# Chunk inverse of an RWKV-7 mixer: levels on diagonal 32x32 blocks, the last level as corner products

## The reference

```
sa = einsum('bhij,bhj->bhi', S, -kk_t)
S  = S * w_t + sa[..., None] * (kk_t * a_t) + v_t[..., None] * k_t
y  = einsum('bhij,bhj->bhi', S, r_t)
```

## Time and profile before

| | |
|---|---|
| median of the runs | 1234.13 us |
| profiled execution | 1235.34 us, of which the span 1233.5 us |
| PE busy, weight loads busy | 1101.8 us (89%), 803.3 us (65%) |
| DVE, ACT, POOL busy | 520.1, 301.7, 132.5 us |
| mean granted TensorE clock | 0.952 of full speed |
| instructions | 25771 |

### The profile page before, as it was taken

The page is one execution under the profiler, slowest core; times in us unless marked ns, Lnnn a source line. Parts: engine busy times, 40 slices in busy tenths (PEclk is TensorE's granted clock), DMA queues, the critical chain, the costliest instruction groups (busy, mean ns, idle before and its releaser), DMA issues.

```text
span 1233.5 us, 25771 instructions
## 1 busy us (share of the span) xinstructions
PE 1101.8 (89%) x11555; PEld 803.3 (65%) x11555; DVE 520.1 (42%) x906; ACT 301.7 (24%) x565; POOL 132.5 (11%) x154
## 2 busy tenths in 40 slices
PE   3469999999999999999787796999999999999994
PEld 1247777868686877778563283888585666665563
DVE  0693346454545445454646906120211254543104
ACT  1103131232322222312202113122211344443011
POOL 0261010010100000100102411000000000100010
PEclk9779999999999999999998898899999899999897
DMA  9400103030302121120506138022211122423001
GB/s 353 180 1 1 70 11 133 2 141 2 141 3 91 53 72 71 33 111 2 206 19 247 54 137 339 32 79 80 90 69 52 69 76 97 172 87 137 1 1 69
DMA packets 18014, 110.46 MB, mean 90 GB/s; under 512 B 6888, under 2 KB 9712, under 8 KB 11760
## 3 DMA queue, kind: packets, MB, share of 16 engines
q1 hardware_dynamic: 10640, 84.57, 18.2%
q0 software_dynamic: 2304, 20.97, 4.5%
q10 hardware_dynamic: 4960, 3.27, 0.9%
HBM read 103.35 MB, written 5.19 MB: 88 GB/s over the span
## 4 chain that ended last, share of the span: by engine, by line
PE 76%; DVE 14%; issue 5%; ACT 3%; DMA 2%; SPq 0%; ACTq 0%; DVEq 0%
PE pj L949 19%; PE bk L1053 9%; PE pj L1370 7%; PE pj L1301 5%; PE pj L1427 3%; DVE XM L1728 3%; PE pj L1297 2%; PE bk L1399 2%; PE bk L1480 2%; PE bk L879 2%; DMA ring<-in_ada 2%; PE bk L1464 1%; PE bk L1465 1%; PE bk L1014 1%; PE bk L1309 1%
## 5 line engine op out<-in xcount | busy, mean ns | idle before, releaser
L949 PE MATMUL pj<-XM,ring 128*128 128x260 f32 x1024 | 256.0, 396 | 7.8 <-DVE XM L1728 7.8
L949 PEld LDWEIGHTS pj<-XM,ring 128*128 128x128 f32 x1024 | 187.2, 191 | 47.5 <-issue 18.6
L1053 PE MATMUL bk<-arena,ring 64*64 64x64 f32 x2560 | 92.7, 222 | 6.3 <-DVE arena L1807 5.5
L1053 PEld LDWEIGHTS bk<-arena,ring 64*64 64x64 f32 x2560 | 81.8, 136 | 24.8 <-issue 15.8
L1370 PE MATMUL pj<-XM,ring 128*128 128x260 f32 x352 | 80.6, 393 | 0.0
L1370 PEld LDWEIGHTS pj<-XM,ring 128*128 128x128 f32 x352 | 68.8, 196 | 11.0
L1813 DVE TENSOR_TENSOR arena<-arena,bk 128x512 f32<-128x512 f32 x40 | 27.5, 688 | 107.6 <-PE bk L1053 107.6
L879 PE MATMUL bk<-ring,cT 128*9 128x512 f32 x240 | 35.1, 685 | 19.6 <-DMA ring<-in_ada 19.6
L1945 DVE TENSOR_SCALAR arena<-bk 128x512 f32<-128x512 f32 x4 | 2.8, 691 | 105.5 <-PE bk L1323 73.7
L2025 DVE TENSOR_TENSOR bk<-bk,arena 128x128 f32<-128x128 f32 x32 | 9.6, 299 | 72.5 <-PE bk L1465 37.3
L1728 DVE SCALAR_TENSOR_TENSOR XM<-R,vecs 128x520 f32<-128x520 f32 x40 | 38.8, 1040 | 0.2
(11 more groups left out here) (343 smaller groups left out, 1854.6 us busy)
## 6 DMA issues: line engine op xcount, KB each, us to landing
ring<-in_ada SPq DMA_DIRECT2D x16, 2048.0 KB, 8.4
ring<-in_w_in SPq DMA_DIRECT2D x8, 2048.0 KB, 7.3
ring<-in_b_w_in SPq DMA_DIRECT2D x3, 2048.0 KB, 16.1
R<-in_xT SPq DMA_DIRECT2D x2, 2080.0 KB, 13.4
ring<-in_w_out SPq DMA_DIRECT2D x2, 2048.0 KB, 8.3
ring<-in_w_q SPq DMA_DIRECT2D x2, 1536.0 KB, 6.4
out_y<-R SPq DMA_DIRECT2D x4, 520.0 KB, 2.7
XM<-in_Sd SPq DMA_DIRECT2D x1, 2048.0 KB, 17.4
```

Of the source, the lines that this page charges most:

```text
L949: last = mm(pj[:, s, a, 0:HALF], w[:, e, k, :], XM[:, e, k, a * HALF:(a + 1) * HALF], start=(k == 0), stop=(k == KT - 1))
L1053: last = mm(bk[r, out, b * C:(b + 1) * C], lhsT[r, b, :], rhs_[r, b, :], start=True, stop=True)
```

## The change

The levels run to a block size of 32 only, and on the diagonal 32x32 blocks alone. The 16 matrices of 64x64 have 32 such blocks; they lie as 128 partitions by 8 blocks of 32 columns, four in the partitions. T and Tm of the levels are `Tq` and `Tm` (256 columns in place of 512), Z is `Zq`. `blocks` now makes 32 matmuls of 32x32 by 32 columns, on the four array tiles of the diagonal. There are four levels (2, 4, 8, 16), each with both products.

The last level is made from corners: `corner_z` multiplies the off-diagonal corner of M with the lower inverted block, DVE negates it, `corner_t` multiplies the upper inverted block with it and, with an identity, also moves the lower block to its place; DVE copies both into the right half of `Tt`, and ACT copies the upper blocks into its left half (`corner`, semaphore `s_Tc`). The other corner of `Tt` is zeroed once at the start. The half projection that stood in level 4 stands between `corner_z` and `corner_t`, and the "cum" part of DVE's preparation of the next pair between DVE's two corner steps.

`chunk_products` and `plain_products` are written in parts, so that the 32x32 blocks come out at the partitions and columns where the levels read them; the masks follow, and one constant, `idq`, is loaded more.

Core of the diff:

```diff
-LEVELS = (2, 4, 8, 16, 32)
+LEVELS = (2, 4, 8, 16)
+QC = 32
...
+            def corner(m):
+                act.wait_ge(s_Te, (NLEV + 2) * m + NLEV + 1)
+                for cp in range(2):
+                    lo = slice(cp * C, cp * C + QC)
+                    last = A(Tt[lo, :, 0:QC], Tq[lo], ACT.Identity)
...
+                mark(last, s_Tc)
...
-                for i in range(2):
-                    for a, x in ((0, Bt), (1, Kt_)):
-                        for cp in range(2):
-                            ch = 2 * (2 * half + i) + cp
-                            for h in range(2):
...
+                halves = [(i, cp, h) for i in range(2) for cp in range(2) for h in range(2)]
+                for i, cp, h in halves:
+                    r, ch = slice(h * HD, (h + 1) * HD), 2 * (2 * half + i) + cp
+                    for q in range(2):
+                        p0 = cp * C + q * QC
+                        mm(bk[p0:p0 + QC, b + h, i * 256:i * 256 + QC], Bt[r, ch * C + q * QC:ch * C + (q + 1) * QC],
+                           AR[v][r, 0, ch, q * QC:(q + 1) * QC], start=True, stop=True)
...
             def blocks(out, lhsT, rhs_):
                 for b in range(BLK):
-                    for cp in range(2):
-                        r = slice(cp * C, (cp + 1) * C)
-                        last = mm(bk[r, out, b * C:(b + 1) * C], lhsT[r, b, :], rhs_[r, b, :], start=True, stop=True)
+                    for q in range(4):
+                        r = slice(q * QC, (q + 1) * QC)
+                        last = mm(bk[r, out, b * QC:(b + 1) * QC], lhsT[r, b, :], rhs_[r, b, :], start=True, stop=True)
...
+            def corner_z(m):
+                pe.wait_ge(s_Te, (NLEV + 2) * m + NLEV + 1)
+                for b in range(BLK):
+                    for cp in range(2):
+                        r, lo = slice(cp * C + QC, (cp + 1) * C), slice(cp * C, cp * C + QC)
+                        last = mm(bk[lo, 0, b * QC:(b + 1) * QC], Mab[r, b, 0:QC], Tq[r, b, :], start=True, stop=True)
...
+            def corner_t(m):
+                pe.wait_ge(s_Ze, (NLEV + 1) * (m + 1))
+                for b in range(BLK):
+                    for cp in range(2):
+                        r, lo = slice(cp * C + QC, (cp + 1) * C), slice(cp * C, cp * C + QC)
+                        mm(bk[lo, 2, b * QC:(b + 1) * QC], Tm[lo, b, :], Zq[lo, b, :], start=True, stop=True)
+                        last = mm(bk[r, 2, b * QC:(b + 1) * QC], id64[r, QC:C], Tq[r, b, :], start=True, stop=True)
...
-                        if l == 4:
-                            project(m + 1, 3, KT // 2, KT)
...
+                corner_z(m)
+                if more:
+                    project(m + 1, 3, KT // 2, KT)
+                corner_t(m)
```

More of the change, by code:

```diff
@@ L142, in build @@
         Q_AB, Q_RB, Q_B, Q_AK, Q_RK, Q_K = range(6)
-        Mab, Tm = (cutX(BLK * C).rearrange("p (b t) -> p b t", b=BLK) for _ in range(2))
+        Mab = cutX(BLK * C).rearrange("p (b t) -> p b t", b=BLK)
+        Tq, Tm = (cutX(BLK * QC).rearrange("p (b t) -> p b t", b=BLK) for _ in range(2))
         adarow = Mab.rearrange("p b t -> p (b t)")
@@ L305, in build @@
         s_Te = sem("inverse_t_stored")
+        s_Tc = sem("inverse_corner_placed")
         s_AT = sem("a_turned")
@@ L669, in _ @@
                         prep(m + 1, part)
+                corner(m)
                 chunk_inputs(m)
@@ L1006, in chunk_products @@
                     pe.wait_ge(s_Soa, m)
-                for i in range(2):
-                    for a, x in ((0, Bt), (1, Kt_)):
-                        for cp in range(2):
-                            ch = 2 * (2 * half + i) + cp
-                            for h in range(2):
[L1012 to L1017, removed]
+                halves = [(i, cp, h) for i in range(2) for cp in range(2) for h in range(2)]
[5 more added lines that the diff above has]
+                           AR[v][r, 0, ch, q * QC:(q + 1) * QC], start=True, stop=True)
+                for i, cp, h in halves:
+                    r, ch = slice(h * HD, (h + 1) * HD), 2 * (2 * half + i) + cp
+                    mm(bk[cp * C:(cp + 1) * C, b + h, i * 256 + C:i * 256 + P], Bt[r, ch * C:(ch + 1) * C],
+                       AR[v][r, 1, ch, :], start=True, stop=True)
+                for i, cp, h in halves:
+                    r, ch = slice(h * HD, (h + 1) * HD), 2 * (2 * half + i) + cp
+                    last = mm(bk[cp * C:(cp + 1) * C, b + h, i * 256 + P:i * 256 + 2 * P], Kt_[r, ch * C:(ch + 1) * C],
+                              AR[v][r, :, ch, :], start=True, stop=True)
+                    if i == 1 and cp == 1:
+                        last.then_inc(s_M, 1)
             def turn_a(m):
@@ L1029, in plain_products @@
                 pe.wait_ge(s_Me, 5 * m + 4)
[L1030 to L1035, removed]
+                for ch in range(NCH):
+                    t, cp = ch // 2, ch % 2
+                    for q in range(2):
+                        for h in range(2):
+                            r, p0 = slice(h * HD, (h + 1) * HD), cp * C + q * QC
+                            last = mm(bk[p0:p0 + QC, h, t * C + (1 - q) * QC:(t + 1) * C],
+                                      AR[v][r, 0, ch, q * QC:(q + 1) * QC], Bt[r, ch * C:ch * C + (q + 1) * QC],
+                                      start=True, stop=True)
                 last.then_inc(s_M, 1)
@@ L1690, in _ @@
             then(V.memset(pj[:, :, :, HALF:512], 0.0), s_bz)
-            then(V.memset(bk[:, 0:2, :], 0.0), s_bz)
+            then(V.memset(bk[:, 0:4, :], 0.0), s_bz)
+            then(V.memset(Tt, 0.0))
             def ada(g):
@@ L1818, in inverse_products, with corner, corner_out @@
+                dve.wait_ge(s_T, n + 2)
+                mark(V.tensor_tensor(Tm, Tm, quarters(1), ALU.subtract))
+            def corner(m):
+                dve.wait_ge(s_Z, (NLEV + 1) * (m + 1))
+                then(V.tensor_scalar(Zq, quarters(0), -1.0, None, ALU.mult), s_Ze)
+            def corner_out(m):
+                dve.wait_ge(s_T, (2 * NLEV + 1) * (m + 1))
+                mark(V.tensor_copy(Tt[:, :, QC:C], quarters(2)), s_Te)
             def inverse_products(m):
@@ L1884, in _ @@
                         prep(m + 1, "ss")
-                    if more and l == 4:
-                        prep(m + 1, "cum")
                     level_t(m, l)
+                corner(m)
+                if more:
+                    prep(m + 1, "cum")
+                corner_out(m)
                 inverse_products(m)
```

63 lines of the change are left out of this document (34 added, 29 removed).

## The result

The changed kernel takes 1250.86 us in the median (1245.05 to 1253.01, four runs), the kernel before beside it 1235.24: a ratio of 1.012 with an interval of 1.0075 to 1.0166. It is slower by some 15 us, where a gain of 3 us was forecast. The time lies above the forecast's own range (1222 to 1238) and inside the wider one (1206 to 1252); the sign is the other one.

A forecast was written before the change was run, and what follows sets the result against it. PE was taken to bound seven pairs, the PE-VectorE round trip the last; 32 us of array gain, 31 us of instruction waits and 2 us gained in the last pair sum to -3, giving 1231 us, range 1222 to 1238.

The forecast's parts named there:

- the forecast's own range: Whole kernel's time, 1222 to 1238 us, from a supply of 3.15 to 3.5 us per line of 256 PE instructions.
- the wider one: Whole kernel's time for 8 in 10, 1206 to 1252 us.
- The bound: PE itself bounds seven full pairs; the round trip between PE and VectorE bounds the last pair.
- The array: PE's work in a full pair: groups of 0.56 us, less new waits and tile changes, gain 4.6 us, in seven 32.
- The rival of narrow waves that don't get shorter: PE's level groups: a group of 64 records stays 0.93 us, supply costs about 10 us, kernel 1251 us; chance 0.20.
- Instructions: PE's program: 12 lines per pair in place of 8, at 3.3 us each; waits cost 4.5 us per pair, 31 in seven.
- The rival that supply hides it: PE's instruction lines come early enough: the 38 us gain stays, less a few, 1196 to 1206 us; chance 0.19.
- -32 + 31 - 2: Whole kernel: 32 us array gain and 31 us instruction waits in seven pairs, 2 us gain in the last; sum -3.
- The last pair: Its inverse: instruction supply holds it at 22.5 us against 24.53 before, a gain of 2 us and not 6.

The follow-up runs named there:

- the fastest kernel: Changed kernel without Tm products, lower blocks of A by transposes, ScalarE copies for corner_t's identity products, projections in smaller pieces behind each Z and T: 1189.66 us.
- the late DVE: Kernel before, with four extra VectorE multiplications of T ahead of its second-level T update in the seven full pairs, so PE pauses: 1255.07 us.
- the kernel with half the level instructions: Changed kernel with each level group as 16 matmuls over 64 columns in place of 32 over 32, part of the computation left out: 1193.32 us.
- the other order: Changed kernel with the same instructions, the next pair's projections cut in quarters and also put between T and Tm: 1223.11 us.
- the wide control: Kernel before with 16 additional 128x128 matmuls over 128 columns per full pair, ahead of the second level's T product: 1259.26 us.
- the shorter pause: Kernel before with two extra VectorE multiplications of T ahead of its second-level T update in the seven full pairs: 1241.25 us.
- the last three: Changed kernel with Tm by VectorE transpose, 1202.34 us; also lower blocks by transposes and copies for identity products, 1197.88; also projections in pieces, 1189.66.
- the shifted one: Changed kernel with 24 additional 32x32 matmuls (96 PE instructions) once, ahead of the first projection: 1237.94 us.
- the burst: Kernel before with 96 additional 32x32 matmuls (384 PE instructions) per full pair, ahead of the second level's T product: 1263.95 us.
- doubled instructions: Kernel before with each 64x64 level matmul cut in two of 32 weight columns, twice the instructions in the level groups: 1254.47 us.

## Why the prediction was wrong

*The bound.* PE in the full pairs, DVE's round trip in the last: right. In the fastest kernel the full pairs are still PE's.

*The array.* 0.56 us for a group, 0.42 for DVE's step and 1.3 from T to Z came out as worked out. A gain of 4.6 us per full pair was forecast. The six windows: 8.3 us longer, less 25.8 for stalls beyond before's, less eight stretches of 3.4 us at 1.45 each (the price from the late DVE), 11.6, leaves 29.1 gained, 4.85 per pair; window 5, which needs no such price, gives 4.8. The rival of narrow waves that don't get shorter is refuted: 64 records in 0.56 us are 8.7 ns apart. That its number, 1251, is the measured one is chance, and so is that the time lies within the wider range, whose upper end was taken from this rival. The Trainium skill, page "TensorE: Matmul & The Clock Gate", section "Wait — 56ns, not 53.3ns?", gives some 25 ns as the least distance of two starts; the trace does not agree for matmuls on four different tiles.

*Instructions.* Twelve lines per pair, 123 packets, two to five "issue" gaps per pair of 0.4 to 2.2 us: right. The forecast had 4.5 us per pair beyond before's; measured are 4.3 (25.8 over 6). The rival that supply hides it is refuted by the stalls, and the kernel with half the level instructions shows the time it would have had. The Trainium skill, page "Runtime: NRT & Kernel Launch", section "Instruction fetch mechanics", has the crossing of a block mostly hidden; that held for the wide projections of before, and not for these groups, where one crossing cost up to 2.66 us (in the changed kernel, pair 0, until 163.06). The packet's end lies 1.2 to 1.6 us before PE's return; 1.3 was forecast.

*The step that failed* is the sum, "-32 + 31 - 2", which has no term for the clock. It took a stall at its own length and let the time after it run at 2.4 GHz, as it did in windows 0 to 5 of before, where no stall was longer than 1.2 us. But a stall of about 2 us is also a pause. In the six windows the clock fell at PE's return or within 1.7 us of it after five of the seven stalls of 1.8 us and more, and after one of 1.67: 27.2 us at 1.2 GHz, 11.6 us of time or 1.9 per pair. That is the size of the miss there: 4.85 gained, 4.3 and 1.9 lost, 1.4 us slower per pair, where 0.1 faster was forecast. Shown for the cause: without the stalls the clock stays (half the instructions), and a pause with neither narrow tiles nor instructions brings it down (the late DVE). The forecast had read a granted clock of 1.00 off pairs whose pauses were shorter and taken it for a constant. The warning stood in its own rows: the last pair of before had 0.91 and 0.93, and PE's timeline there shows why.

```profile
615.89 1.90 PE L1053 MATMUL bk<-arena,ring 64*64 64x64 f32 x32 [3.88 <-DVE arena L1807]
617.52 1.98 PE L1053 MATMUL bk<-ring,arena 64*64 64x64 f32 x32
```

Behind a pause of 3.88 us these groups start 1.63 us apart in place of 0.98, which is 1.2 GHz.

*The last pair.* A gain of 2 was forecast, and it lost 2.9. Its stalls are 10.0 us, since no projection stands between the bursts, and 17.2 us run at 1.2 GHz against 6.8 before. Its inverse takes 28.1 us (623.17 to 651.29), where 22.5 was forecast from supply; that bound left both out, and the waits for DVE that stand between the stalls. How much each of them makes there is not shown. Stalls and clock were also left out for the inverse of pair 0, which was counted like the others: stalls of 2.1, 0.8 and 2.7 us and 6.8 us at 1.2 GHz.

*What stays open:* what decides whether a given pause is followed by a fall. No kernel whose pauses there stay under 1.5 us (before, half the instructions, the other order, the wide control, the shorter pause, and the last three) has time at 1.2 GHz in windows 0 to 5. Of the stalls and made pauses of 1.8 us and more, from the inverse of pair 0 to the end of window 5, seven of nine had the clock down behind them in the changed kernel and five of six in the shifted one, both with the burst, two of seven equal ones with the late DVE, and not the single one (1.97 us) with doubled instructions. Of six stalls of 1.5 to 1.8 us (in the changed, the doubled and the burst kernel) one had it, the 1.67. And all thirteen kernels wait once for DVE ahead of pair 0's transposes of b and k (`turn_bk`, in before until 128.58), 2.6 us from matmul to matmul and nearly the same in all; the clock fell behind it in four (half the instructions, the other order, the burst, and the fastest) and not in nine. So neither the length of the pause nor the work around it decides alone. That the short stalls and narrow groups around a pause make a fall likelier fits the counts, but no run separates it.

## What to carry to other kernels

Before matmuls are made smaller, count PE's instructions in a row: where the work between two long instructions takes less time than its lines take to come (here 3.3 us per 256), the array time that is saved turns into stalls, and a stall near 2 us can cost as much again through the clock (1.45 us for each stretch of 3.4 us at 1.2 GHz here). Cut the instructions or spread them between long ones; here a transpose on an idle engine and another order turned a loss of 15 us into a gain of 44. Read the granted clock stage by stage, and do not carry its value over to a version with longer pauses.

## What the runs showed of the hardware that was not expected

Ninety-six instructions added at the start made the kernel 13 us faster, by moving the ends of lines in the work. Seven pauses of 1.99 us, at the same place in the work of seven pairs, were followed by 1.2 GHz twice, and a pause of 2.6 us that all thirteen kernels have was in four; so this loss varies with the moment. And a wave of four matmuls of 32 columns on four tiles takes 35 ns (0.56 us over 16), so that matmuls start 8.7 ns apart; the densest in the trace of before were 14.5 ns apart.
